# Pairing the attention steps of a two-layer hybrid diffusion backbone, and loading the vectors ahead of the input rows

## The reference, cut to what matters

```python
def layer(x, mod, p, ...):
    h = rms_norm(x, p["g_pre_mix"]) * (1.0 + sc1) + sh1      # sh1, sc1, ... from silu(c) @ w_mod + b_mod
    y, ... = mixer(h, p, ...)
    x = x + g1 * rms_norm(y, p["g_post_mix"])
    h = rms_norm(x, p["g_pre_ffn"]) * (1.0 + sc2) + sh2
    x = x + g2 * rms_norm(swiglu(h, p), p["g_post_ffn"])

def attend(q, k, v):                                          # 8 heads, blocks of 128 queries
    s = einsum("bqhd,bkhd->bhqk", q, k) * 96 ** -0.5
    return einsum("bhqk,bkhd->bqhd", softmax(s), v)

def mixer(...):                                               # only its end
    y_mla = attend(q, k, v) @ p["w_o_mla"]
    y_lru = ((hf_seq + hb_seq) * gelu(lru_gate)) @ p["w_o_lru"]
    y = (gates[..., :D] * y_mla + gates[..., D:] * y_lru) @ p["w_out"]
```

## Time and profile before

| | |
|---|---|
| median of 3 runs | 1308.81 us |
| the profiled execution itself | 1308.53 us |
| its span | 1305.7 us |
| TensorE busy | 1275.4 us, 98% of the span |
| VectorE, ScalarE busy | 62%, 51% |
| 16 DMA engines, mean | 46.9% of their time, 150 GB/s |

### The profile page before, as it was taken

The page is one execution under the profiler, slowest core; times in us unless marked ns, Lnnn a source line. Parts: engine busy times, 40 slices in busy tenths (PEclk is TensorE's granted clock), DMA queues, the critical chain, the costliest instruction groups (busy, mean ns, idle before and its releaser), DMA issues.

```text
span 1305.7 us, 20057 instructions
## 1 busy us (share of the span) xinstructions
PE 1275.4 (98%) x7715; PEld 1175.4 (90%) x7715; DVE 813.2 (62%) x1413; ACT 661.1 (51%) x1170; POOL 18.2 (1%) x38
## 2 busy tenths in 40 slices
PE   5999999999999999999999999999999999999998
PEld 4999999978889999998789999998897999999886
DVE  2697584764769877643368785747566885444424
ACT  4479873754454332342266888547444543333322
POOL 0000000200000000000000000001000000000000
PEclk9999999999999999999999999999999999999999
DMA  9645645333426766534325545463324464443531
GB/s 335 200 131 158 210 129 200 111 99 113 145 90 206 220 200 210 161 130 156 103 65 161 147 153 181 143 214 114 113 66 146 133 212 129 129 130 129 170 105 65
DMA packets 135058, 196.21 MB, mean 150 GB/s; under 512 B 9730, under 2 KB 68268, under 8 KB 134964
## 3 DMA queue, kind: packets, MB, share of 16 engines
q1 hardware_dynamic: 134964, 194.94, 46.9%
HBM read 193.03 MB, written 1.88 MB: 149 GB/s over the span
## 4 chain that ended last, share of the span: by engine, by line
PE 88%; ACT 5%; DVE 4%; issue 2%; DMA 0%; SPq 0%; DVEq 0%; ACTq 0%
PE bank L671 18%; PE bank L678 18%; PE bank L679 18%; PE bank L766 5%; PE bank L765 5%; PE bank L764 5%; ACT sq L1192 2%; PE bank L710 2%; DVE weight_low L1564 1%; PE bank L631 1%; PE bank L1058 1%; PE bank L1082 1%; PE bank L746 1%; ACT weight_high L1184 1%; PE bank L1067 1%
## 5 line engine op out<-in xcount | busy, mean ns | idle before, releaser
L678 PE MATMUL bank<-act_low,weight_high 128*128 128x384 f32 x1440 | 486.7, 338 | 0.6 <-DVE weight_low L1564 0.6
L679 PE MATMUL bank<-act_high,weight_low 128*128 128x384 f32 x1440 | 482.4, 335 | 0.0
L1564 DVE TENSOR_TENSOR weight_low<-raw,weight_high 128x1024 fp32r<-128x1024 f32 (+5 forms) x282 | 319.2, 1152 | 173.8 <-ACT weight_high L1184 173.4
L1184 ACT ACTIVATE weight_high<-raw 128x1024 fp32r<-128x1024 f32 (+5 forms) x282 | 273.2, 996 | 241.0 <-PE bank L766 73.7
L671 PE MATMUL bank<-act_high,weight_high 128*128 128x384 f32 x1440 | 315.1, 339 | 1.8 <-DVE t L1668 1.8
L678 PEld LDWEIGHTS bank<-act_low,weight_high 128*128 128x128 f32 x1440 | 270.7, 188 | 6.6 <-issue 4.9
L679 PEld LDWEIGHTS bank<-act_high,weight_low 128*128 128x128 f32 x1440 | 271.0, 188 | 0.0
L671 PEld LDWEIGHTS bank<-act_high,weight_high 128*128 128x128 f32 x1440 | 252.2, 188 | 8.4 <-issue 5.7
L764 PE MATMUL bank<-weight_high,hid_high 128*128 128x512 f32 x264 | 104.4, 395 | 0.0
L766 PE MATMUL bank<-weight_high,hid_low 128*128 128x512 f32 x264 | 102.8, 389 | 0.0
L765 PE MATMUL bank<-weight_low,hid_high 128*128 128x512 f32 x264 | 102.8, 389 | 0.0
(11 more groups left out here) (241 smaller groups left out, 1542.8 us busy)
## 6 DMA issues: line engine op xcount, KB each, us to landing
raw<-in_w_ffn_in SPq DMA_DIRECT2D x176, 256.0 KB, 3.8
mod_weight<-in_w_mod SPq DMA_DIRECT2D x80, 512.0 KB, 4.8
raw<-in_w_in SPq DMA_DIRECT2D x72, 512.0 KB, 4.0
raw<-in_w_ffn_out SPq DMA_DIRECT2D x44, 512.0 KB, 3.8
first_mod<-in_w_mod SPq DMA_DIRECT2D x4, 2048.0 KB, 13.9
raw<-in_w_o_lru SPq DMA_DIRECT2D x16, 512.0 KB, 3.8
raw<-in_w_out SPq DMA_DIRECT2D x16, 512.0 KB, 3.7
raw<-in_w_o_mla SPq DMA_DIRECT2D x8, 512.0 KB, 4.8
```

What stands on the lines that cost most here:

```text
L678: nc.tensor.matmul(o, view[0][:, kk, cols], low[:, k, :], start=False, stop=False)
L679: ins = nc.tensor.matmul(o, view[1][:, kk, cols], high[:, k, :], start=False, stop=k == total - 1)
L1184: nc.scalar.activation(high, w, ACT.Copy).then_inc(*AC.step())
L1564: nc.vector.tensor_tensor(low, w, high.bitcast(F), ALU.subtract).then_inc(*VE.step())
```

## The change

TensorE's attention work comes in pairs: `attention_pair(s)` for even s issues values(s-2), turn(s), scores(s+2), scores(s+3), turn(s+1). Five pairs stand at places 8, 13, 18, 22 and 27 of `ol0`, one between the jobs, six at 4, 9, 14, 19, 24 and 28 of `ol1`; turn(23) follows at place 31. VectorE takes the two maxima of a pair first, then the two divisions, then the low parts that belonged to either step. `mix_lru(0)` now stands ahead of the maximum of step 12. ScalarE's order is the same. On SyncE, c_ctx, c, the identity and fold go ahead of the two loads of x.

```diff
         def _(sp):
-            sp.dma_start(x[:, 0, :], A["x_prompt"]...).then_inc(start_x[0], 16)
-            sp.dma_start(ident[:, :], A["ident"]).then_inc(start_load, 16)
-            sp.dma_start(x[:, 1:3, :], A["x_sample"]...).then_inc(start_x[1], 16)
             sp.dma_start(cache_c[0:C, 0:P], A["c_ctx"]...).then_inc(start_load, 16)
             sp.dma_start(cache_c[C:2 * C, 0:P], A["c"]...).then_inc(start_load, 16)
+            sp.dma_start(ident[:, :], A["ident"]).then_inc(start_load, 16)
             sp.dma_start(fold[:, :], A["fold"]).then_inc(start_fold, 16)
+            sp.dma_start(x[:, 0, :], A["x_prompt"]...).then_inc(start_x[0], 16)
+            sp.dma_start(x[:, 1:3, :], A["x_sample"]...).then_inc(start_x[1], 16)
...
-                def attention_step(s):
+                def attention_pair(s):
+                    if s >= 2:
+                        values(s - 2)
+                    turn(s)
                     if s + 2 < 24:
                         scores(s + 2)
-                    turn(s)
-                    if s >= 2 and s % 2 == 0:
-                        values(s - 2)
+                        scores(s + 3)
+                        turn(s + 1)
...
-                split_job("ol0", ..., between=attention_steps(0))
-                attention_step(12)
-                split_job("ol1", hh, hl, between=attention_steps(13), bank_free=(VE, "mix_lru"))
+                split_job("ol0", ..., between=attention_pairs({8: 0, 13: 2, 18: 4, 22: 6, 27: 8}, begin=3))
+                attention_pair(10)
+                split_job("ol1", hh, hl, between=attention_pairs({4: 12, 9: 14, 14: 16, 19: 18, 24: 20, 28: 22}, end=31),
+                          bank_free=(VE, "mix_lru"))
...
-                for s in range(24):
+                def maximum(s):
                     n = TP if head_tile(s)[1] == 0 else TK - TP
                     ve.wait_ge(*at(PE, "scores", s))
                     nc.vector.tensor_reduce(negmax[...], bank("attn", s % 2)[:, 0:n], AX.X, ALU.max, negate=True)
+                for s in range(0, 24, 2):
+                    if s == 12:
+                        mix_lru(0)
+                    maximum(s)
                     if s >= 8 and (s - 8) % 6 == 0:
                         out_low((s - 8) // 6)
-                    if s >= 1:
-                        divide(s - 1)
-                    if s == 13:
-                        mix_lru(0)
-                    ...            # lows() by s
-                divide(23)
+                    maximum(s + 1)
+                    divide(s)
+                    divide(s + 1)
+                    for e in (s, s + 1):
+                        ...        # the same lows() by e
```

More of the change, by code:

```diff
@@ L437, in _ @@
         def _(sp):
[L438 to L440 removed]
             sp.dma_start(cache_c[0:C, 0:P], A["c_ctx"].rearrange("(n p) -> n p", p=P)).then_inc(start_load, 16)
             sp.dma_start(cache_c[C:2 * C, 0:P], A["c"].rearrange("b (n p) -> (b n) p", p=P)).then_inc(start_load, 16)
+            sp.dma_start(ident[:, :], A["ident"]).then_inc(start_load, 16)
             sp.dma_start(fold[:, :], A["fold"]).then_inc(start_fold, 16)
+            sp.dma_start(x[:, 0, :], A["x_prompt"].rearrange("b t d -> (b t) d")).then_inc(start_x[0], 16)
+            sp.dma_start(x[:, 1:3, :], A["x_sample"].rearrange("b (a p) d -> p (b a) d", p=P)).then_inc(start_x[1], 16)
             def first_mods(rs):
@@ L1128, in merged_first, with attention_pairs @@
                     PE.also("used", loads[1])
-                def attention_steps(first):
-                    start = 0 if first else 4
+                def attention_pairs(places, begin=None, end=None):
                     def between(i, count):
-                        if i == start - 1:
+                        if i == begin:
                             attention_begin()
[L1137 to L1141, removed]
-                    return between
-                split_job("ol0", hh, hl, ready=(VE, "lru_low"), ready_high=(AC, "lru_high"), between=attention_steps(0))
-                attention_step(12)
-                split_job("ol1", hh, hl, between=attention_steps(13), bank_free=(VE, "mix_lru"))
+                        if i in places:
+                            attention_pair(places[i])
+                        if i == end:
+                            turn(23)
+                    return between
+                split_job("ol0", hh, hl, ready=(VE, "lru_low"), ready_high=(AC, "lru_high"),
+                          between=attention_pairs({8: 0, 13: 2, 18: 4, 22: 6, 27: 8}, begin=3))
+                attention_pair(10)
+                split_job("ol1", hh, hl, between=attention_pairs({4: 12, 9: 14, 14: 16, 19: 18, 24: 20, 28: 22}, end=31),
+                          bank_free=(VE, "mix_lru"))
                 merged_first()
@@ L2036, in _ @@
                                             ).then_inc(*VE.step("max", s))
+                for s in range(0, 24, 2):
+                    if s == 12:
+                        mix_lru(0)
+                    maximum(s)
                     if s >= 8 and (s - 8) % 6 == 0:
                         out_low((s - 8) // 6)
-                    if s >= 1:
-                        divide(s - 1)
-                    if s == 13:
-                        mix_lru(0)
[L2043 to L2048, removed]
-                divide(23)
+                    maximum(s + 1)
+                    divide(s)
+                    divide(s + 1)
+                    for e in (s, s + 1):
+                        if e in (2, 4):
+                            lows("ol0", 1 + e // 2)
+                        elif e == 6:
+                            lows("ol1", 0)
+                        elif e >= 8 and e % 3 == 2:
+                            lows("ol1", 0, ahead=min(e, 9) // 3 + max(e - 13, 0) // 3 - (1 if e == 8 else 0))
                 out_low(3)
```

## The result

The changed kernel took 1312.9 us, the median of 14 runs (1311.11 to 1314.28); the kernel before, run beside it, 1309.35 us (14 runs, 1307.06 to 1312.91). The ratio is 1.0018 with a 95% interval of 1.0011 to 1.0026: 2.4 us slower, between 1.4 and 3.4. The profiled execution took 1311.46 us, its span 1309.6. The median lies inside the forecast range of 1302.5 to 1313.0, at its upper end, and within 0.3% of the kernel before.

What follows compares the result with a forecast made beforehand. TensorE, busy 98% of the span, was taken as the bound. Attention +0.9 us a layer, +1.8 for two, and the opening -1.2 gave +0.6 on 1308.53: 1309.1, or 1309.4 as a median; range 1302.5 to 1313.0.

Steps and rivals of the forecast that it cites:

- second rival: Between ol0 and ol1, TensorE's stall also loses the clock in both layers: 1.6 us a layer, 1313.8 us; chance 0.15.
- The six waits go: In attention, six steps' transposes (2, 4, 6, 8, 10, 11) no longer wait after the scores: -2.9 us a layer.
- The copy wait: In pairs 4, 10 and 16, turn(s+1) waits 0.4 us for ScalarE's copy of turn(s): +1.2 us a layer.
- The border: Between ol0 and ol1, TensorE waits for banks that VectorE's late mix_lru(0) frees: +3.3 us a layer, ends 0 and 4.
- first rival: Between ol0 and ol1, VectorE is in time and nothing stalls: -2.4 us a layer, 1302.8 us; chance 0.25.
- Value products: In attention, 11 value groups a layer now exit to transposes, saving 0.08 us each: -0.9 us, between 0 and -2.2.
- The opening: At program start, earlier c lets ScalarE's chain start sooner, capped by w_mod's landing: 1.2 us gained, ends 0 and 2.5.
- third rival: In attention, waits only move and a 1.7 us border stall cancels 2.9; w_mod holds the opening: 1308.8 us; chance 0.12.

Runs made afterwards that it cites:

- the pairs alone: The changed kernel with the old order of first loads on SyncE; 1316.52 us, ratio 1.0041 to the kernel before.
- both repairs: Changed kernel with mix_lru(0) before divide(11) and turn(5), turn(11), turn(17) one place later: 1301.19 us; with opening fillers too, 1298.73 us.

## Why the prediction came out

The forecast was 1309.4 us and no change beyond 0.3%; 1312.9 was measured, in the range and within 0.3%, but 3.5 us above the forecast. 0.5 of that is the base (before at 1309.35, not 1308.81). The time itself lies nearer to the second rival's 1313.8. By the forecast's own steps, per layer:

- **The six waits go, -2.9.** Right: no turn(s) of an even step waits in the profile after.
- **The copy wait, 0.4 each in pairs 4, 10 and 16, +1.2.** Right: 0.31 between the end of the scores and the transposes, 0.35 to 0.37 each by what their removal gave back, +1.1.
- **The border, +3.3.** Right in place, order and size: 2.45 us until the first bank and 0.8 at VectorE's pace, 3.2 at the full clock. Moving `mix_lru(0)` ahead of divide(11) removes all of it; moving it ahead of the two lows removes their part. The first rival (no stall) is out.
- **The clock behind the border.** This was the second rival, not the forecast, with 0.15: it came true in both layers. By its own sum it cost 1.6 us a layer; it cost 1.1 and 1.0, shown by filling the border. The Trainium skill, "TensorE: Matmul & The Clock Gate", section "HAM oscillation", tells of gaps that put the engine back on the half clock; both borders of the profile agree (0.51), though the section tells it of longer waits than the 2.4 us here. The forecast's step that failed is here: it took the stall's price as its length alone. The row was there: 1.81 us of idle time had been followed by a stretch at half clock, and the wait at the border was to be longer.
- **Value products, -0.9.** Half to two thirds of that: the pairs cost some 0.05 us less than the sum of their parts, 0.5 to 0.6 in a layer.
- Sum per layer with the measured terms: -2.9 + 1.1 + 3.2 + 1.1 - 0.6 + 0.2 = +2.1; the profile shows +2.3 and +2.05, and with the pairs alone +2.7 and +2.2. In that layer 0 the clock fell later and nine products were slow instead of six, which makes the clock's term 1.5 and the sum 2.5; 0.2 is left. Not all of the time is explained either: two layers of 2.1 to 2.7 make 4.3 to 4.9 us, the pairs alone measured +5.4, with an interval (3.7 to 7.2) that holds them.
- **The opening, -1.2.** The two times that were to move earlier did so (L639 at 3.49, forecast 4.5; L844 at 14.66, forecast 15.6). L671 came at 29.11 and not near 28.2: what was late next was not a wait but the clock; with fillers ahead of them the same products took 1.92 us again and L671 came at 27.05. So by the two profiles -0.4. Over runs it is -3.8 (-5.1 to -2.5), beyond the end of 2.5 that the forecast gave. The term was mis-sized because it was taken from one execution of before at the fast end: of four profiles of the old order the three others are 1.6 to 4.5 us later at the same instruction in attention, by a later c, by the clock, or by both, while the six of the new order with no filled opening lie between -1.1 and +0.4. The forecast had put the clock of the opening at nothing in either order.

The pairs were forecast at +1.8 and measured at +5.4 (3.7 to 7.2), the opening at -1.2 and measured at -3.8. The two errors, +3.6 and -2.6, have opposite signs and for the most part cancel. The mechanism of the waits was right, the clock's stood in a rival and not in the forecast, and that the sum came out in the range is in good part luck. The third rival, waits only moved and nothing from the opening, is out: it had a border stall of 1.7 where 3.2 were measured, and both halves are clear of zero.

## What to carry to other kernels

Before work is regrouped on the bounding engine, price one passage by a lone group in the trace; here it was free, and all that the regrouping gave or took came from who waits for whom. When a step of another engine is put behind others in its order (here four multiplications behind two low parts of 1.1 us), follow it to the bank that it frees: one line moved turned +0.18% into -0.68%. A stall is priced with the clock that may follow it, and the start of a program is compared over runs and over several profiles, not by one.

## What the runs showed of the hardware

- Idle time of TensorE had a second price. After 2.4 us without a product the granted clock was 0.51 for 3.4 us, in both layers and in each of the two profiles with that border; it fell between 0.0 and 1.3 us after the first product behind the gap had started. With ten useless products in the gap, or with only four slow products and no such gap (1.58 us for 0.79 of work), it stayed at 1.00.
- A float32 product between products in fp32r costs its own 0.22 us at full width; one of 64 columns of the array costs 0.35 us more each time that it is entered and left, measured over 15 passages.
- The same 16 products of the first w_mod block took 1.92, 1.92, 2.88 and 2.89 us in the four profiles of the old order, 3.64 in the six of the new order, and 1.92 with fillers ahead of them.
- Three loads of 4 to 64 KB that stood first on the queue had landed by 3.4 to 3.5 us in all seven profiles of that order; the 4 KB of c behind loads of 0.5 and 1 MB landed between 7.7 and 10.3 us.
- The changed kernel with both repairs and the opening filled scattered by 0.35 us over 4 runs; the kernel before by 3.5 to 5.9 over 8 to 21.
